# Attention maps kept negated, their least value used as the bias; two maps in one VectorE operation, and the gates' products in one

## The reference

```python
# nsa (first block), selected keys and window keys: two maps for each head
s = einsum(q, k) * ATTN_SCALE                      # 64 ** -0.5 = 0.125
out = gc[..., 0:1] * o_cmp + gc[..., 1:2] * o_slc + gc[..., 2:3] * o_win
# dsa (second block, layer 0): 8 heads, the best 64 keys of each query
s = s * scale + bias_a[rel_bucket(dist)];  p = softmax(s)
# diff (layer 0): 4 heads with two maps each
a = probs(q1, k1) - lam * probs(q2, k2)
# forgetting (layer 1): 16 heads
s = s * scale + cq[..., :, None] - cum[..., None, :];  p = softmax(where(causal, s, -1e30))
```

## Time and profile before

| | |
|---|---|
| time, median of 3 runs | 2415.68 us (2414.46 to 2417.91) |
| profiled execution | 2415.85 us, its span 2414.2 us |
| busy share | PE 71%, DVE 65%, POOL 46%, ACT 16% |
| chain that ended last | PE 36%, DVE 24%, DMA 21%, POOL 10%, issue 7%, ACT 2% |
| moved by DMA | 757.93 MB, mean 314 GB/s; from slice 15 of 40 on nearly always 350 to 410 GB/s |
| attentions (us) | nsa 157 to 281, even0 751 to 782, even1 940 to 1030, odd0 1365 to 1440, odd1 1776 to 1856 |

### The profile page before, as it was taken

One profiled execution on the slowest core, in us unless ns is written; L12 is line 12 of the kernel. 1 busy time (PEld: TensorE's weight loads), 2 busy tenths in 40 slices (PEclk: granted clock), 3 DMA queues, 4 the chain that ended last, 5 costly groups with the idle time before them and its releaser, 6 DMA issues.

```text
span 2414.2 us, 23581 instructions
## 1 busy us (share of the span) xinstructions
PE 1723.7 (71%) x7282; PEld 1194.6 (49%) x7282; DVE 1567.2 (65%) x3525; ACT 388.0 (16%) x999; POOL 1100.5 (46%) x1124
## 2 busy tenths in 40 slices
PE   6999968999797737768568466865757776255556
PEld 5887757888685723345237235523623552011112
DVE  3328533630215689877995786798479689877774
ACT  1012511100112112311011221111122111000001
POOL 1001100200000046766765576676557667777773
PEclk9889989999997869889879787988978898587888
DMA  8646625975341589999999999999999999999996
GB/s 291 212 139 222 199 96 173 381 250 152 96 132 52 161 316 369 396 409 409 406 360 406 384 374 404 409 394 358 409 358 379 409 409 377 386 410 409 409 409 244
DMA packets 210158, 757.93 MB, mean 314 GB/s; under 512 B 23036, under 2 KB 26248, under 8 KB 209800
## 3 DMA queue, kind: packets, MB, share of 16 engines
q0 software_dynamic: 161280, 587.27, 62.9%
q1 hardware_dynamic: 48344, 167.35, 19.6%
q10 hardware_dynamic: 432, 2.03, 0.2%
HBM read 755.50 MB, written 1.07 MB: 313 GB/s over the span
## 4 chain that ended last, share of the span: by engine, by line
PE 36%; DVE 24%; DMA 21%; POOL 10%; issue 7%; ACT 2%; POOLq 0%; DVEq 0%; ACTq 0%; SPq 0%
PE psL L467 27%; DMA W<-experts_v,crow 13%; POOL W L458 10%; DVE W L973 8%; DMA W<-experts_u,crow 6%; PE psO L467 4%; DVE Z L903 3%; PE psS L467 2%; PE psT L467 2%; DMA wring<-weights 1%; DVE N L903 1%; DVE N L906 1%; DVE Sb L903 1%; DVE mx L1050 1%; DVE Z L909 1%
## 5 line engine op out<-in xcount | busy, mean ns | idle before, releaser
L467 PE MATMUL psL<-W,con 128*128 128x512 f32 x1072 | 607.1, 706 | 360.3 <-DMA W<-experts_v,crow 317.4
L458 POOL DMA_INDIRECT W<-experts_u,crow x512 | 525.4, 1026 | 561.5 <-DVE crow L906 336.9
L973 DVE SCALAR_TENSOR_TENSOR W<-W,psL 128x1024 f32<-128x1024 f32 x512 | 609.2, 1217 | 194.0 <-DMA W<-experts_u,crow 191.8
L458 POOL DMA_INDIRECT W<-experts_v,crow x512 | 524.0, 1023 | 265.4 <-issue 133.7
L467 PEld LDWEIGHTS psL<-W,con 128*128 128x128 f32 x1072 | 218.9, 221 | 698.8 <-issue 605.8
L467 PE MATMUL psL<-N,wring 128*128 128x256 f32 x1744 | 399.9, 391 | 22.5 <-DVE N L903 12.5
L467 PEld LDWEIGHTS psL<-N,wring 128*128 128x128 f32 x1744 | 338.4, 196 | 77.1 <-issue 11.6
L903 DVE SCALAR_TENSOR_TENSOR Z<-W,crow,Z 128x1024 f32<-128x1024 f32 x240 | 307.8, 1282 | 52.5 <-DMA W<-experts_v,crow 46.4
L441 POOL DMA_DIRECT2D W<-ada x96 | 50.9, 530 | 453.4 <-DVE W L1103 452.6
L1545 ACT ACTIVATE con<-con,crow 128x128 f32<-128x128 f32 x268 | 102.2, 396 | 576.9 <-PE psL L467 330.8
L467 PE MATMUL psO<-N,wring 128*128 128x128 f32 x928 | 127.9, 296 | 63.7 <-DVE N L906 50.9
(11 more groups left out here) (213 smaller groups left out, 1533.0 us busy)
## 6 DMA issues: line engine op xcount, KB each, us to landing
wring<-weights SPq DMA_DIRECT2D x311, 512.0 KB, 6.2
W<-ada POOLq DMA_DIRECT2D x96, 512.0 KB, 6.0
W<-experts_u,crow POOLq DMA_INDIRECT x512, 9.0
W<-experts_v,crow POOLq DMA_INDIRECT x512, 9.0
W<-rel_rows SPq DMA_DIRECT2D x1, 1536.0 KB, 9.0
X<-x_dram ACTq DMA_DIRECT2D x1, 1024.0 KB, 5.7
out<-N SPq DMA_DIRECT2D x1, 1024.0 KB, 3.9
W<-rel_rows SPq DMA_DIRECT2D x1, 768.0 KB, 4.9
```

The source lines that it names most:

```text
L458: pool.indirect_dma_start(W[:, slot * D:(slot + 1) * D], None, experts_u if kind == "u" else experts_v, bass.IndirectOffsetOnAxis(ap=idx[: ...
L467: return pe.matmul(o, l, r, start=first, stop=last)
L973: dve.scalar_tensor_tensor(out=row, in0=row, scalar=1.0, in1=hps, op0=ALU.mult, op1=ALU.mult, accum_out=dots[:, col:col + 1]).then_inc(row ...
```

## The change

Sb now holds the negative of the scores: each operation multiplies by -0.125 and subtracts its bias, and the selection mask is subtracted too. The least value of a row of Sb is then the negative of the greatest score, which is what exp needs as its bias, so TENSOR_REDUCE takes the minimum, and the TENSOR_SCALAR that negated `mx` is gone (48 operations). ACT's exp reads Sb with a scale of -1. In the late attentions one SCALAR_TENSOR_TENSOR over both banks of psS replaces two (24 jobs); in all dsa jobs one TENSOR_TENSOR replaces two (8 jobs); in nsa one product with both gates replaces two (16 jobs). In nsa and even0 the two SCALAR_TENSOR_TENSORs stay. DVE issues 96 operations fewer.

```diff
-                    for m in range(2):
-                        ins = stt(Sb[:, b, m * S:m * S + w], score(kind, n, m, w), 0.125, jb["bias"][m],
-                                  ALU.mult, ALU.add)
+                    s3 = Sb[:, b, :].rearrange("p (m w) -> p m w", m=2)[:, :, 0:w]
+                    b3 = jb["bias"] if jb["kind"] == "dsa" else jb["bias"][:, None, :].to_broadcast([P, 2, w])
+                    if kind in LATE:
+                        ins = stt(s3, psS[:, :, 0:w], -0.125, b3, ALU.mult, ALU.subtract)
+                    else:
+                        for m in range(2):
+                            ins = stt(s3[:, m, :], score(kind, n, m, w), -0.125, b3[:, m, :], ALU.mult, ALU.subtract)
                     link(ins)
                     if jb["kind"] == "dsa":
-                        for m in range(2):
-                            s = Sb[:, b, m * S:m * S + w]
-                            ins = tt(s, s, sel[T][:, 0:w], ALU.add)
-                        link(ins)
-                    link(dve.tensor_reduce(mx[:, b, 0:2], Sb[:, b, :].rearrange("p (m w) -> p m w", m=2)[:, :, 0:w],
-                                           AX.X, ALU.max))
-                    ts(mx[:, b, 2:4], mx[:, b, 0:2], -1.0, None, ALU.mult).then_inc(smax_ready, 1)
+                        link(tt(s3, s3, sel[T][:, None, 0:w].to_broadcast([P, 2, w]), ALU.subtract))
+                    dve.tensor_reduce(mx[:, b, 0:2], s3, AX.X, ALU.min).then_inc(smax_ready, 1)
...
-                    for m in range(2):
-                        if jb["fac"][m] is not None:
-                            ins = tt(facs[:, b, m:m + 1], facs[:, b, m:m + 1], jb["fac"][m], ALU.mult)
-                    if any(f is not None for f in jb["fac"]):
-                        link(ins)
+                    if jb["fac"] is not None:
+                        m = 2 - jb["fac"].shape[1]
+                        link(tt(facs[:, b, m:2], facs[:, b, m:2], jb["fac"], ALU.mult))
...
                         ins = f(Pb[:, b, m * S:m * S + w], Sb[:, b, m * S:m * S + w], ACT.Exp,
-                                bias=mx[:, b, 2 + m:3 + m], accum_out=sums[:, b, m:m + 1])
+                                bias=mx[:, b, m:m + 1], scale=-1.0, accum_out=sums[:, b, m:m + 1])
```

More of the change, by code:

```diff
@@ L344, in causal, with relbias @@
             return con[:, CON["causal"] + P * (1 - T):CON["causal"] + S]
-        def relbias(h, T):
-            return bias0[:, h * P:(h + 1) * P] if T == 0 else bias1[:, h * S:(h + 1) * S]
+        def relbias(h, T, n=1):
+            return bias0[:, h * P:(h + n) * P] if T == 0 else bias1[:, h * S:(h + n) * S]
         jobs = []
@@ L354, in build @@
                 jobs.append(dict(kind="nsa", T=T, rows=[rows, rows], q=[ZQ + j] * 2, k=[ZKS, ZKW],
-                                 bias=[causal(T)] * 2,
-                                 fac=[G[:, T, 3 * h + 1:3 * h + 2], G[:, T, 3 * h + 2:3 * h + 3]],
+                                 bias=causal(T), fac=G[:, T, 3 * h + 1:3 * h + 3],
                                  v=[lambda kt: VT[:, kt * P:(kt + 1) * P],
@@ L363, in build @@
                                  q=[EQA + j] * 2, k=[24 + j] * 2,
-                                 bias=[relbias(2 * j, T), relbias(2 * j + 1, T)], fac=[None, None],
+                                 bias=relbias(2 * j, T, 2).rearrange("p (m w) -> p m w", m=2), fac=None,
                                  v=[lambda kt, j=j: VT[:, kt * 512 + j * P:kt * 512 + (j + 1) * P]] * 2,
@@ L369, in build @@
                 jobs.append(dict(kind="diff", T=T, rows=[slice(0, 64), slice(64, 128)],
-                                 q=[EQB + h] * 2, k=[EKB + h] * 2, bias=[relbias(8 + h, T)] * 2,
-                                 fac=[None, tiny[:, 60:61]],
+                                 q=[EQB + h] * 2, k=[EKB + h] * 2, bias=relbias(8 + h, T),
+                                 fac=tiny[:, 60:61],
                                  v=[lambda kt, h=h: VT[:, 1024 + kt * 512 + h * P:1024 + kt * 512 + (h + 1) * P]] * 2,
@@ L376, in build @@
                 jobs.append(dict(kind="forget", T=T, rows=[slice(0, 64), slice(64, 128)],
-                                 q=[OQ + j] * 2, k=[OK + j] * 2, bias=[causal(T)] * 2, fac=[None, None],
+                                 q=[OQ + j] * 2, k=[OK + j] * 2, bias=causal(T), fac=None,
                                  v=[lambda kt, j=j: VT[:, kt * 1024 + j * P:kt * 1024 + (j + 1) * P]] * 2,
```

## The result

The changed kernel took 2402.75 us (median of 5 runs, 2401.56 to 2409.57), the kernel before 2417.91 us in the same session. The ratio is 0.9943 with a 95% interval of 0.9926 to 0.996, so by the ratio 13.8 us were saved, 9.7 to 17.9. I had forecast 6.7 us, 2409.0 with a range of 2405.0 to 2413.2. The direction was right, the size half of it. The profiled execution of the changed kernel took 2402.75 us.

A forecast was written before the change was run, and what follows sets the result against it. PE bounds most of nsa, a serial DVE-PE loop even0, DVE-coupled gathers the late attentions, then DMA. Savings of 1.3, 1.8, 0.7, 1.3 and 1.5 us (unrounded 6.66, so 6.7) give 2409.0 us, range 2405.0 to 2413.2.

The forecast's parts named there:

- nsa: 5 x (0.19 + 0.07) = 1.3: In nsa, the start and four fronts with their scales on DVE's stretch save 1.3 us; other jobs lie under PE.
- even0: 8 x 0.19 + 4 x 0.07 = 1.8: In even0, all eight fronts are in one serial loop, so the removed DVE time saves 1.8 us.
- Negation 0.19, joins 0.07, minimum and scale -1 for nothing: DVE saves 0.19 us per removed negation and 0.07 per joined pair; minimum and exp's scale -1 cost nothing extra.
- even1 0.7: In even1, two dsa fronts ahead of the row freeing a gather slot save 0.7 us; six jobs lie under DMA.
- odd0 1.3: In odd0, two fronts before the slot-freeing row save 0.5 us, three more 0.8 passed on through the hold.
- odd1 1.5: In odd1, 0.5 us at the restart and 1.0 from six fronts in full loops, 0.26 - 0.09 each.
- The hold: In odd1, a gather begun during DVE's Z accumulation finishes only 2.08 us after that began, coupling POOL to DVE's loop.
- rival 4: In odd1, the hold catches one gather more per loop: 2.7 us slower, 2418.4; chance 0.05.
- Late sum 3.6: even1, odd0 and odd1 together save 0.7 + 1.3 + 1.6 = 3.6 us.
- 1: Gathers keep pace in odd0 and odd1 loops whatever DVE does, or joins give nothing: 4.9 us saved, 2410.8; chance 0.16.
- 2: Only what lies before the gathers counts, DMA takes the rest: 3.1 us saved, 2412.6; chance 0.14.
- 3: Jobs put under PE, DMA and row waits pass time on too, all 48 fronts: 12.5 us saved, 2403.2; chance 0.09.

The follow-up runs named there:

- e3_nsa: The change in nsa only (negation removed, gates joined in 16 jobs), the rest as in the kernel before: 2499.88 us, ratio 0.999.
- e5_even0: The change in even0 only (negation removed in 8 jobs, mask operations joined in 4), the rest as in the kernel before: 2494.43 us, ratio 0.9968.
- c_after: The whole changed kernel again, on another chip, against the kernel before: 2489.65 us, ratio 0.994.
- c2_after: The whole changed kernel once more, in a later session, against the kernel before: 2490.98 us, ratio 0.9941.
- e4_late: The change in even1, odd0 and odd1 only (24 jobs), nsa and even0 as in the kernel before: 2499.96 us, ratio 0.998.
- c_before: The kernel before itself, unchanged, run for a profile on the chip of the other runs of its call: 2498.65 us.
- e2_join: Only the joined score, mask and gate operations, with the negation kept, against the kernel before: 2498.94 us, ratio 0.9979.
- late half: The change in even1, odd0 and odd1 only, against the kernel before: saved 4.2 +- 4.1 us, with e4_late weighted in 3.9 +- 3.2.
- e9_dose_hidden: The changed kernel plus four idle operations in each of 16 fronts in nsa, even1 and odd0 forecast to count nothing, against the kernel before: 2490.02 us, ratio 0.9954.
- early half: The change in nsa and even0 only, against the kernel before: 2492.24 us, ratio 0.9954, saved 9.4 +- 3.9 us.

## Why the prediction was wrong in size

The step that failed is the pair of terms "nsa: 5 x (0.19 + 0.07) = 1.3" and "even0: 8 x 0.19 + 4 x 0.07 = 1.8" as the whole gain ahead of the gathers, with the sentence "what follows an attention is a fixed chain". 3.1 were forecast. 6.4 were measured at the first gather (means of five and seven traces), and 9.4 +- 3.9 at the end. The work in them was nearly right, 1.48 and 1.87. What I left out is that PE's clock is no constant: the earlier trace rows show it at 0.92 in nsa and 0.57 in even0, and I priced everything but DVE's part as fixed. Where PE waits less, stretches at half clock go or move. Of the other 3.0 us, 1.5 are in nsa, and there the clock is shown as the cause, by seven executions against thirteen and by e3_nsa. That the clock costs time in even0 and behind it is shown by filling PE's waits (1.00 and 3.5 us), but the change itself left even0's rounds at 0.50, and the 0.6 behind even0 is missing in three of seven executions. The 0.4 at the start lies ahead of the change. The 0.6 between nsa and even0 go with nsa's change (484.50 us in e3_nsa, 485.45 in e5_even0, of which its own front took 0.27), but what passes them on is only argued.

The Trainium skill, TensorE: Matmul & The Clock Gate, section "HAM oscillation — how this bites in real kernels", describes a matmul kernel whose waits between bursts of matmuls put PE back to the slower clock, and the time lost there. The trace agrees: 0.50 from 754.4 us to the end of even0, and 1.00 from 759.7 us on when the waits are filled.

Point by point:
- *Negation 0.19, joins 0.07, minimum and scale -1 for nothing:* right, in every round of nsa and even0 (3.78 to 3.52; 691, 424, 553 and 446 ns).
- *even1 0.7:* the restart came 7.1 us sooner and the first gather 6.6, so 0.5.
- *odd0 1.3:* pause 0.52 shorter, rounds 9.22 to 8.95. Right by these places; what the stream of gathers kept of it can't be told from one pair (above).
- *odd1 1.5:* pause 0.52 shorter. The loop went from 10.00 to 9.75 and not to 9.83, so there the 0.09 that I let the scaling pair give back did not come. But the last two rounds gave 0.12 and -0.14, and from first to last exp odd1 became 1.35 us shorter, in all near my 1.5. On the other chips odd1 is less even: in c_after, c2_after and e4_late one of its rounds takes 14.8 to 14.9 us and the next 6.6 to 7.2, in c_before none over 11.5. No run isolates that.
- *The hold:* right, and it passed the time on. POOL and DVE in odd1 of the changed kernel:

```profile
1791.78 1.94 POOL L457 DMA_INDIRECT W<-experts_v,crow  x1 [0.30 <-DVE W L972]
...
1798.99 0.98 POOL L457 DMA_INDIRECT W<-experts_u,crow  x1 [0.30 <-issue]
...
1801.53 1.93 POOL L457 DMA_INDIRECT W<-experts_u,crow  x1 [0.31 <-DVE W L972]
```

```profile
1791.63 1.28 DVE L902 SCALAR_TENSOR_TENSOR Z<-W,crow,Z 128x1024 f32<-128x1024 f32 x1
1792.83 0.68 DVE L902 SCALAR_TENSOR_TENSOR Sb<-psS,con 128x512 f32<-128x512 f32 x1
...
1797.89 1.28 DVE L902 SCALAR_TENSOR_TENSOR Z<-W,crow,Z 128x1024 f32<-128x1024 f32 x1
```

The long gathers begin 9.75 apart with seven in the loop, the first ends 2.09 after the accumulation began, and the gather at 1798.99 lies 1.10 behind the next accumulation and is hardly held (0.98). So rival 4, one gather more caught, did not come.
- *Late sum 3.6:* measured 3.9 +- 3.2.
- *Rivals:* 1 falls with the joins at 691 and 424 and the pace of POOL, though in e2_join's odd1 the join was worth nothing. The rule cited for it, from the Trainium skill, VectorE: DVE Perf Modes, section "Rules for kernel authors", goes on to ask for fewer operations, with which the 0.07 agree, so that worth 0 does not follow from it; 2 (nothing behind the first gather) falls with the two pauses that became shorter, and lies outside the late half's bounds (0.7 to 7.1); 3 had the right time, 2403.2, for a wrong reason, as e9_dose_hidden shows.

In the first pair the 13.1 us of the two profiles are 6.6 at the first gather, 3.6 more up to the last gather, which is what I had forecast for the late part, and 2.9 behind it. What stays open: whether the early half is worth 6.4 us, as at the first gather, or up to 13, as its bounds allow; and these 2.9 us behind the last gather, where its rows landed after 7.73 us instead of 10.24. One pair of executions can't tell that from scatter.

## What to carry to other kernels

When an operation leaves a loop in which PE waits for DVE, count its time once, and then ask what PE's granted clock is in that loop and behind it: a loop with a clock under 1.00 can give back more than was removed, here about as much again up to the first gather, in steps that differ from one execution to the next. Compare places in the traces before the total: rounds ahead of the gathers agreed to 0.01 or 0.02 us where the clock was the same, and the first gather to 3.4, where the total scattered by 20 and more. And a total that a rival had right is no evidence for that rival until its own places have been tried.

## What the runs showed of the hardware

- Matmuls that nobody reads made a serial loop faster: with such a group in each of even0's eight jobs its later rounds fell from 3.05 to 2.50 us, with PE at clock 1.00; a round before that, at 0.50, grew from 3.51 to 4.01.
- The same kernel took 2416 to 2418 us on one chip and 2501 to 2504 on three others. Ahead of the gathers there is hardly a difference (first gather at 841.76 and 844.86). Behind it the DMA-bound stretch moved 409 GB/s on the first chip and 373 in c_before:

```profile
2120.00:2360.00 240.00, 129.01 (x195) 42.73 (x196) 171.17 (x233) 18.82 (x54) 182.65 (x189) 0.83 1.03 409
```

```profile
2120.00:2360.00 240.00, 107.47 (x149) 34.93 (x150) 169.95 (x255) 17.17 (x47) 173.44 (x172) 0.67 0.98 373
```

- A chained 128x2 TENSOR_SCALAR cost DVE 0.20 us in even0 (four add 0.81 to a round, twenty 4.06). Beside the gathers of odd1 it was 0.20 with four to a front (0.80) and 0.23 with twelve (2.74).
